# Attention queries and keys computed token-stationary and turned through memory, and the softmax weights turned by sixteen transfers, in a two-layer fp32 trunk on one core

## What is computed

```python
def _moba_mixer(x, w_qkv, w_out):
    qkv = (x @ w_qkv).reshape(bsz, seqlen, 3, ATTN_HEADS, ATTN_HEAD_DIM)
    q, k, v = qkv[:, :, 0], qkv[:, :, 1], qkv[:, :, 2]
    q = (_partial_rope(q, cos, sin) * (ATTN_HEAD_DIM ** -0.5))   # rotates 32 of 128
    k = _partial_rope(k, cos, sin)
    ...
    p = jax.nn.softmax(s, axis=-1)      # s: q k over the selected and the own block
    ...
    return o @ w_out                    # o = p v
```

## Time and profile before

| what | us |
|---|---|
| three runs, median (lowest to highest) | 2096.89 (2096.42 to 2096.99) |
| profiled execution, its own time | 2096.86 |
| its span | 2095.04 |
| TensorE busy | 2085.9 |
| DVE busy | 1290.4 |
| ACT busy | 975.1 |

### The profile page before, as it was taken

The page is one execution under the profiler, slowest core; times in us unless marked ns, Lnnn a source line. Parts: engine busy times, 40 slices in busy tenths (PEclk is TensorE's granted clock), DMA queues, the critical chain, the costliest instruction groups (busy, mean ns, idle before and its releaser), DMA issues.

```text
span 2095.0 us, 28820 instructions
## 1 busy us (share of the span) xinstructions
PE 2085.9 (100%) x9918; PEld 1749.5 (84%) x9918; DVE 1290.4 (62%) x1246; ACT 975.1 (47%) x1172; POOL 21.3 (1%) x16
## 2 busy tenths in 40 slices
PE   9999999999999999999999999999999999999999
PEld 8898888888888888888988888888888888888887
DVE  6869666665555565555766667675665554555565
ACT  5596455434444443443644445454434443443442
POOL 0000010000000000000000000010000000000000
PEclk9999999999999999999999999999999999999999
DMA  7665758766766766775654556658666766766763
GB/s 257 195 197 189 235 180 261 250 200 203 236 222 183 238 230 201 219 233 171 193 186 158 168 167 225 202 189 267 216 210 212 241 206 195 243 218 228 241 212 120
DMA packets 233547, 439.80 MB, mean 210 GB/s; under 512 B 15056, under 2 KB 37840, under 8 KB 232432
## 3 DMA queue, kind: packets, MB, share of 16 engines
q1 hardware_dynamic: 232032, 432.79, 65.2%
q10 hardware_dynamic: 1424, 5.77, 0.7%
HBM read 419.63 MB, written 18.87 MB: 209 GB/s over the span
## 4 chain that ended last, share of the span: by engine, by line
PE 99%; DMA 0%; ACT 0%; issue 0%; DVE 0%; ACTq 0%
PE ps L427 75%; PE ps L419 11%; PE ps L416 5%; PE ps L726 1%; PE ps L725 1%; PE ps L724 1%; PE ps L558 1%; PE ps L739 0%; DMA wst<-in_rg_w_in_dram 0%; PE ps L524 0%; PE ps L523 0%; PE ps L525 0%; PE ps L596 0%; PE ps L714 0%; PE ps L599 0%; PE ps L575 0%
## 5 line engine op out<-in xcount | busy, mean ns | idle before, releaser
L1014 DVE TENSOR_TENSOR wl<-wst,wh 128x1024 fp32r<-128x1024 f32 x743 | 887.8, 1219 | 327.3 <-ACT wh L757 324.0
L757 ACT ACTIVATE wh<-wst 128x1024 fp32r<-128x1024 f32 x743 | 769.8, 1059 | 649.1 <-PE ps L427 411.8
L427 PE MATMUL ps<-wh,hid 128*128 128x512 f32 x2560 | 695.9, 390 | 0.0
L427 PEld LDWEIGHTS ps<-wh,hid 128*128 128x128 f32 x2560 | 479.5, 188 | 98.9
L427 PE MATMUL ps<-wh,xin 128*128 128x512 f32 x2048 | 548.9, 389 | 0.0
L427 PEld LDWEIGHTS ps<-wh,xin 128*128 128x128 f32 x2048 | 383.9, 188 | 79.4
L427 PE MATMUL ps<-wl,hid 128*128 128x512 f32 x1280 | 404.6, 389 | 0.0
L419 PE MATMUL ps<-xin,wh 128*128 128x512 f32 x960 | 331.2, 395 | 0.8 <-DVE wl L1014 0.8
L427 PE MATMUL ps<-wl,xin 128*128 128x512 f32 x1024 | 315.2, 389 | 0.0
L427 PEld LDWEIGHTS ps<-wl,hid 128*128 128x128 f32 x1280 | 240.2, 188 | 50.0
L416 PE MATMUL ps<-xin,wl 128*128 128x256 f32 x960 | 256.8, 278 | 0.0
(11 more groups left out here) (138 smaller groups left out, 835.9 us busy)
## 6 DMA issues: line engine op xcount, KB each, us to landing
wst<-in_mlp_w_dram SPq DMA_DIRECT2D x512, 512.0 KB, 4.7
wst<-in_moba_w_qkv_dram SPq DMA_DIRECT2D x96, 512.0 KB, 4.6
wst<-in_rg_w_in_dram SPq DMA_DIRECT2D x62, 512.0 KB, 4.1
wst<-in_rg_w_out_dram SPq DMA_DIRECT2D x32, 512.0 KB, 4.9
sq_by_quad<-f SPq DMA_DIRECT2D x128, 128.0 KB, 2.5
f<-sq_by_quad SPq DMA_DIRECT2D x32, 512.0 KB, 5.1
wst<-in_moba_w_out_dram SPq DMA_DIRECT2D x32, 512.0 KB, 5.3
f<-in_x_dram SPq DMA_DIRECT2D x8, 256.0 KB, 6.3
```

The lines of the kernel that those rows point to most:

```text
L427: return pe.matmul(banks(half)[:, a, :], src[:, c, part, a * P:(a + 1) * P], (wl if low else wh)[:, s, w], start=(c == 0 and part + low == 0),
L757: act.activation(wh[:, off % SPLITS, :], wst[:, slot, :], ACT.Copy).then_inc(wh_done, 1)
L1014: dve.tensor_tensor(wl[:, off % SPLITS, :], wst[:, off % STAGE, :], wh[:, off % SPLITS, :], ALU.subtract).then_inc(wl_done, 1)
```

## The change

1. Q and K turns become `token_turn`. ACT evicts each in two pieces into `qk_out`; SP stores it (four transfers) and reads it back to `qk_quad` through the same scratch; DVE turns it and then rotates. `take_hl` and `add_hh` are gone from this part.
2. The softmax weights are no longer turned by TensorE. DVE scales them into `prob_out` in parts of 32 columns, sixteen transfers of 32 partitions x 384 (48 KB) move them within SBUF, eight issued by SP and eight by ACT, and DVE turns the squares.
3. The score matmuls move to the last block of the V turn, and the product with V to the second block of the next group's K turn; for the last group it goes to place 8 of the output projection, whose first two turns are now interleaved (`W2_ORDER`, as in the MLP). The exponentials and all behind them move into the next group's Q turn.
4. The first Q turn begins token-stationary. The loops over groups on SP, ACT and DVE are written out.

```diff
+            def store_qk(g, part):
+                sp.wait_ge(qk_evict, HALVES * (2 * g + part + 1))
+                if 2 * g + part:
+                    sp.wait_ge(qk_ready, 2 * g + part)
+                for i in range(GROUP):
+                    sp.dma_start(to_quad[i], qk_out[i * 32:(i + 1) * 32, :, :]).then_inc(qk_stored, 16)
...
+            def move_p(g):
+                sp.wait_ge(p_ready, g + 1)
+                for dst, src in part_moves(prob_quad, prob_out, (0, 1)):
+                    sp.dma_start(dst, src).then_inc(p_moved, 16)
...
             load_rows(1)
-            with sp.Fori(0, NG) as t:
+            for n, (t, kb) in enumerate(W2_ORDER):
+                if n == 2:
+                    store_qk(NG - 1, 1)
+                if n == 3:
+                    read_qk(NG - 1, 1)
+                if n == 2 * BLOCKS - 2:
+                    move_p(NG - 1)
+                load_block(cols_of(moba_w_out[0], t * COLS)[kb], n, B_MO + n)
...
+            for g in range(NG):                                   # TensorE
+                b = B_QKV + 3 * g * BLOCKS
+                own, other = 2 * (g % 2), 2 * (1 - g % 2)
+                if g == 0:
+                    begun_token_turn(1, b, R_LN1)
+                else:
+                    pe.wait_ge(qk_evict, HALVES * 2 * g)
+                    token_turn(xin, own, b, R_LN1)
+                    pe.wait_ge(v_stored, g)
+                token_turn(xin, other, b + BLOCKS, R_LN1, {1: lambda: weighted(g - 1)} if g else {})
+                pe.wait_ge(qk_evict, HALVES * (2 * g + 1))
+                token_turn(xin, own, b + 2 * BLOCKS, R_LN1, {BLOCKS - 1: lambda: scores(g)})
...
+            for g in range(NG):                                   # DVE
+                b = B_QKV + 3 * g * BLOCKS
+                if g:
+                    splits(b, START, START + 1)
+                    softmax_end(g - 1)
+                    splits(b, START + 1, LATE)
+                    turn_p(g - 1)
+                    splits(b, LATE, NEXT)
...
+                b += BLOCKS
+                splits(b, START, START + 2)
+                if g:
+                    weighted_lo(g - 1)
+                rotate(g, 0, qg)
+                splits(b, START + 2, START + 3)
+                rotated(g, 0, qg)
+                splits(b, START + 3, NEXT)
+                b += BLOCKS
+                rotate(g, 1, kg)
+                rotated(g, 1, kg)
+                splits(b, START, LATE + 1)
```

More of the change, by code:

```diff
@@ L438, in token_turn @@
                             for a in range(HALVES):
-                                mm = token_step(src, half, a, c, part, low)
+                                mm = token_step(src, first, a, c, part, low)
                     mm.then_inc(mm_done, 1)
@@ new lines, in take_qk @@
+            def take_qk(g, part, first):
+                act.wait_ge(mm_done, B_QKV + (3 * g + part + 1) * BLOCKS)
+                if part == 0 and g:
+                    act.wait_ge(pt_ready, g)
+                if part:
+                    act.wait_ge(qk_back, 16 * (2 * g + 1))
+                for a in range(HALVES):
+                    by_part = qk_out.rearrange("p q (c a r) -> p a c q r", c=GROUP, a=HALVES)[:, a]
+                    by_col = ps[:, first + a, :].rearrange("p (c q r) -> p c q r", c=GROUP, q=GROUP)
+                    act.activation(by_part, by_col, ACT.Copy).then_inc(qk_evict, 1)
@@ new lines, in exponentials, with move_p @@
+            def exponentials(g):
+                act.wait_ge(bias_ready, g + 1)
+                for h in range(GROUP):
+                    for a, cols in enumerate((slice(0, P), slice(P, 3 * P))):
+                        ex = act.activation(prob[:, h, cols], prob[:, h, cols], ACT.Exp, scale=QK_SCALE,
+                                            bias=stat[:, h, 2 + a:3 + a], accum_out=stat[:, h, 4 + a:5 + a])
+                ex.then_inc(exp_done, 1)
+            def move_p(g):
+                act.wait_ge(p_ready, g + 1)
+                for dst, src in part_moves(prob_quad, prob_out, (2, 3)):
+                    act.dma_start(dst, src).then_inc(p_moved, 16)
```

365 lines of the change are left out of this document (183 added, 182 removed).

## The result

The changed kernel takes **2108.9 us** (median of 4, 2107.25 to 2109.81), the kernel before 2096.8: a ratio of 1.0056 [1.0044, 1.0068]. It is slower by 0.56%, where 2090.4 was forecast; the slowest case that the prediction had priced was 2102.8. The profiled execution took 2108.77 (span 2106.9), 11.91 more than the one of before.

A forecast was written before the change was run, and what follows sets the result against it. TensorE, 99% of the chain of waits, was taken to bound the kernel: 2096.86 - 11.1 of saved work + 4.6 of last-group waits = 2090.4 us; range 2088.5 to 2092 (chance 0.42), with 8 of 10 between 2085.4 and 2099.

The forecast's parts named there:

- the slowest case that the prediction had priced: Attention's softmax-weight moves at 0.92 us an issue: a loss of 12.4 us, time 2102.8.
- What TensorE saves: TensorE's attention work: token-stationary turns make a group 70.66 us; work falls by 11.1 us in all.
- K's way to the scores: K's eviction, store, read, transpose and rotation in the V turn: keys ready at E+17.2, wanted at E+19.05, 1.8 to spare.
- E: The start of a V turn, from which the prediction counts its times in us.
- the spare of 0.4: Time left before the scores when K's trip through memory takes as long as the slowest MLP case of 32, 10.9 us.
- The weights' way to the product: Softmax-weight relay on three engines: done at E+47.6, TensorE there at E+48.9, 1.3 us to spare in the first three groups.
- I take 0.41: Issue price in us of one softmax-weight transfer within SBUF; eight take 3.3 us on ACT.
- slower: the issue of the moves: Rival: dearer softmax-weight issues on ACT delay groups; 2100.9 us at 0.86 each; chance 0.13, shared with SP queue jams.
- y: Issue time of one softmax-weight move above 0.41 us; groups lose 3 (8y - 1.3), the last 8y.
- The clock: Rival: after the last stall, 4 us at 1.2 GHz lose 2 us, giving 2092.4; chance 0.10.
- The last group: Last attention group: earlier product and 2 MB ahead of K's stores cost 3.2 + 1.4 = 4.6 us; bounds 0 to 9.6, or 2 more.
- The moves' number and their landing: Sixteen softmax-weight moves within SBUF overlap, cost mainly issue time and land 2.5 us after issue.

The follow-up runs named there:

- the relay ahead: Against the changed kernel: softmax-weight steps put ahead of splits that stood between them, gain and bias loaded ahead of the first group; 2088.07 us, ratio 0.9950.
- the run by way of memory: Against the changed kernel: softmax weights sent through memory by four stores and one read on SP, replacing sixteen transfers; 2115.77 us, ratio 1.0095.

## Why the prediction was wrong

**What TensorE saves** was right. The kernel whose waits are nearly gone (the relay ahead) has a profiled execution of 2088.19, and 2096.86 - 11.1 + 2.2 of waits is 2088.0. The kernel before ran 1.6 slower beside it (2098.45), so this agreement is partly luck; the group's 70.68 against 70.66 is the firmer sign.

**K's way to the scores** was right in size and wrong in its spread. The keys were ready at E+17.4 in the first group (E+17.2). But the spare of 0.4 "in the slowest case" came from the MLP, where no rotation and no moves hold VectorE up. Where TensorE doesn't stall before, K took up to 22.2 us behind the eviction with 17.75 given. The rows of the MLP could not show this burst.

**The weights' way to the product** is the step that failed. In the first group E is 1047.9:

| link, us behind E | forecast | measured |
|---|---|---|
| mask begins | 25.5 | 26.8 |
| scaling ends | 37.3 | 38.6 |
| ACT's eight issues end | 40.6 | 44.4 |
| ACT's four splits end | 44.5 | 48.5 |
| VectorE's last split ends | 45.7 | 50.3 |
| transpose ends | 47.6 | 52.0 |
| TensorE is there | 48.9 | 49.0 |

The term that was mis-sized is "I take 0.41, since 32 rows of 1.5 KB are fewer pieces than a store's 128". Fewer pieces were not cheaper: the median is 0.59 on SP and 0.62 on ACT, and eight take 5.85 on ACT in the first group and 5.30 in the others. That is 2.6 of the 4.4 us by which the relay was late there, and 2.0 in the others. Another 1.3 are the mask's, which stood behind splits whose loads were late, and 0.5 VectorE's pace. The rival "slower: the issue of the moves" had the mechanism and the formula. With y = 2.55 / 8 in the first group and 2.0 / 8 in the others it gives (2.55 - 1.3) + 2 (2.0 - 1.3) + 2.0 = 4.7, so 2095.1. It lacked the other links, (14.8 - 4.6 - 4.7) / 4 = 1.4 a group, and the clock. Of the 18.4 us between the forecast and the profiled execution, the issues by this formula make 4.7, the other links 5.5 and the clock 7.2, and 1.0 stays open.

**The clock** had a chance of its own with 2 us, for one wait. It came three times and cost 7.2. The slow rows of the start pointed the right way, though the granted clock reads 1.00 there and does not show that they are the same thing. The price was too small because only one wait was forecast. The Trainium skill, "TensorE: Matmul & The Clock Gate", Why this matters for your kernels, warns of such gaps, and this case's trace agrees: the granted clock was 0.50 behind waits of 2.65, 2.98 and 7.05 us, and 1.0 behind one of 1.70.

**The last group** waited 7.05 and 0.41 us, together 2.9 more than the 4.6 that were forecast. Eight issues make 2.0 of it. The 2 MB held K's stores up by 3, as forecast, but the read behind them landed early, so only 0.41 came before the scores and not 1.4. They held up the weight blocks as well: the mask stands behind ACT's splits and their loads, and it began 6.9 us behind the last scores, against 4.3 to 5.2 in the other groups and 5.2 where the 2 MB were loaded elsewhere. That way was not in the forecast.

**The moves' number and their landing.** That sixteen moves would overlap and cost mainly issue time was right: each landed 2.0 us behind its issue at the median, where 2.5 was forecast. The price lay with the engine that issues. The Trainium skill, "DMA: Bandwidth & Descriptors", Rules for kernel authors, advises to join small transfers. The runs bear that out in part: with four moves in place of sixteen the time was 15.7 us less, but that kernel left the rest of the data out. No run joined the moves within SBUF, and the one that sent the weights by memory in five larger transfers was slower.

## What to carry to other kernels

A DMA's issue is work of the engine that issues it: take its price from a row of the same kind of transfer, and where there is none, let the upper bound decide whether the change is worth making, where several of them lie between two links of a relay. In a relay, every link must stand ahead of the work that can wait; here moving one link alone only put the work it displaced, and the loads behind that, in the way of the next. And price a stall of TensorE above its length: here 14.8 us of waits came with 7.2 more for the slow clock.

## What was not expected of the hardware

- A transfer of 32 rows of 1.5 KB within SBUF took 0.51 us or more to issue, with medians of 0.59 (SP) and 0.62 (ACT), more than a store of 128 KB to memory at 0.43, and landed in 2.0. On one queue or on two at once, the price was the same.
- The granted clock fell to 0.50 (1.2 GHz) behind waits of 2.65, 2.98 and 7.05 us, for 3.4 to 6.8 us, and stayed at 1.0 behind one of 1.70. In the other kernels it fell behind waits of 2.70 us and more, with one exception (3.32 in the run by way of memory), and behind none up to 2.50. The longest slow stretches were 10.2 us, in three other kernels. With throwaway work in the wait it never fell.
- A matmul of 128 columns in FP32 showed as two records, 0.23 us in all from start to start, where a transpose of as many columns was one record of 0.12 (1.48 for twelve).
- The executions of kernels with such waits spread more: 2105.56 to 2111.40 for one of them, and 2085.66 to 2091.14 even for the one with the relay ahead, while those of before stay within 1.6 us of one another in each set. That fits waits that depend on when loads land, but wasn't tested.
